# High and low input halves as one 512-column matmul in a two-block transformer kernel, with three changes of order

## What is computed

```python
# first block
xn = _rms(x, norm_attn)
fq, fk, fv, f_logit, nq, kc, vc, ks, vs, kw, vw, nsa_gate, gate_a, gate_b = split(xn @ w_in)
o_a = fox_attention(...)        # 8 heads of 128, decayed softmax
o_b = nsa_attention(...)        # 8 heads, compressed, selected and window branches
merged = sigmoid(gate_a) * (o_a @ w_up_fox) + sigmoid(gate_b) * (o_b @ w_up_nsa)
x = x + merged @ w_out
hn = _rms(x, norm_ffn)
x = x + (silu(hn @ w_ffn_gate) * (hn @ w_ffn_up)) @ w_ffn_down     # d_ff 5632
# second block, on 272 tokens: h = h + rmsnorm(mixer(rmsnorm(h))) for two mixers
#   group-query attention, 8 key groups, gated, then @ attn_w_out
#   gated linear attention, 4 heads, forward and backward, then @ gla_w_out
return h[:, 16:]
```

## Time and profile before

| | us |
|---|---|
| median of 3 runs | 2478.36 |
| lowest, highest | 2477.81, 2478.53 |
| profiled execution, its own time | 2478.49 |
| span of the profile | 2476.7 |
| mean granted TensorE clock | 0.995 |

### The profile page before, as it was taken

How to read it: one execution, slowest core, us unless ns; L and a number is a source line. 1 busy time by engine, 2 the same in 40 slices (tenths; PEclk the granted TensorE clock), 3 DMA queues, 4 the chain that set the end, 5 groups by cost and what they waited for, 6 DMA issues and landing times.

```text
span 2476.7 us, 50606 instructions
## 1 busy us (share of the span) xinstructions
PE 2440.7 (99%) x19618; PEld 2390.2 (97%) x19618; DVE 1474.9 (60%) x2213; ACT 1170.3 (47%) x1654; POOL 90.2 (4%) x117
## 2 busy tenths in 40 slices
PE   9999999999999999999999999999999989999997
PEld 8999999999999999999999999999999979999997
DVE  6666867655665555455554556555565466755655
ACT  6555554433545444334433445554454345545542
POOL 0000000000011000000000001000000100000001
PEclk9999999999999999999999999999999999999998
DMA  7546884466666666666666657655554545645553
GB/s 257 160 154 170 235 208 116 119 173 171 178 191 176 190 181 192 186 181 187 182 192 176 189 161 211 174 140 156 143 158 118 165 112 154 164 136 143 153 154 101
DMA packets 750272, 415.20 MB, mean 168 GB/s; under 512 B 44368, under 2 KB 738640, under 8 KB 750160
## 3 DMA queue, kind: packets, MB, share of 16 engines
q1 hardware_dynamic: 749328, 411.29, 59.3%
q10 hardware_dynamic: 832, 2.36, 0.2%
HBM read 408.35 MB, written 2.10 MB: 166 GB/s over the span
## 4 chain that ended last, share of the span: by engine, by line
PE 92%; DVE 4%; issue 2%; ACT 2%; DMA 0%; DVEq 0%; ACTq 0%; SPq 0%
PE ps_unit L254 27%; PE ps_unit L252 27%; PE ps_unit L253 27%; DVE w_lo L238 1%; PE ps_score L1018 1%; ACT w_hi L231 1%; PE ps_norm L863 0%; PE ps_out L863 0%; DVE work L355 0%; DMA raw<-in_w_fox 0%; PE ps_score L585 0%; PE ps_score L586 0%; DVE work L2548 0%; PE ps_score L842 0%; PE ps_score L817 0%
## 5 line engine op out<-in xcount | busy, mean ns | idle before, releaser
L238 DVE TENSOR_TENSOR w_lo<-raw,w_hi 128x1024 fp32r<-128x1024 f32 (+1 forms) x748 | 875.6, 1211 | 232.7 <-ACT w_hi L231 232.2
L231 ACT ACTIVATE w_hi<-raw 128x1024 fp32r<-128x1024 f32 (+1 forms) x768 | 777.0, 1042 | 440.6 <-PE ps_unit L254 436.8
L252 PE MATMUL ps_unit<-b_hi,w_hi 128*128 128x256 f32 (+1 forms) x3168 | 905.4, 286 | 2.0 <-DVE w_lo L238 2.0
L254 PE MATMUL ps_unit<-b_hi,w_lo 128*128 128x256 f32 (+1 forms) x3168 | 900.4, 284 | 0.0
L253 PE MATMUL ps_unit<-b_lo,w_hi 128*128 128x256 f32 (+1 forms) x3168 | 898.9, 284 | 0.0
L252 PE MATMUL ps_unit<-a_hi,w_hi 128*128 128x256 f32 (+1 forms) x2736 | 778.0, 284 | 3.8 <-DVE w_lo L238 3.4
L253 PE MATMUL ps_unit<-a_lo,w_hi 128*128 128x256 f32 (+1 forms) x2736 | 772.2, 282 | 0.0
L254 PE MATMUL ps_unit<-a_hi,w_lo 128*128 128x256 f32 (+1 forms) x2736 | 772.1, 282 | 0.0
L252 PEld LDWEIGHTS ps_unit<-b_hi,w_hi 128*128 128x128 f32 x3168 | 597.9, 189 | 7.5 <-issue 5.1
L254 PEld LDWEIGHTS ps_unit<-b_hi,w_lo 128*128 128x128 f32 x3168 | 598.5, 189 | 0.0
L253 PEld LDWEIGHTS ps_unit<-b_lo,w_hi 128*128 128x128 f32 x3168 | 595.7, 188 | 0.7
(11 more groups left out here) (385 smaller groups left out, 1704.4 us busy)
## 6 DMA issues: line engine op xcount, KB each, us to landing
raw<-in_attn_w_in SPq DMA_DIRECT2D x96, 512.0 KB, 4.8
raw<-in_gla_w_in SPq DMA_DIRECT2D x96, 512.0 KB, 4.5
raw<-in_w_in SPq DMA_DIRECT2D x88, 512.0 KB, 4.8
raw<-in_w_ffn_gate SPq DMA_DIRECT2D x88, 512.0 KB, 4.8
raw<-in_w_ffn_up SPq DMA_DIRECT2D x88, 512.0 KB, 4.8
raw<-in_w_fox SPq DMA_DIRECT2D x64, 512.0 KB, 4.3
raw<-in_w_ffn_down SPq DMA_DIRECT2D x64, 512.0 KB, 4.6
raw<-in_w_out SPq DMA_DIRECT2D x32, 512.0 KB, 4.5
```

The source lines that it names most:

```text
L231: act.activation(hi[:, b % 4, 0:size], raw[:, b % 8, 0:size], ACT.Copy)\
L238: dve.tensor_tensor(lo[:, b % 4, 0:size], raw[:, b % 8, 0:size], hi[:, b % 4, 0:size], ALU.subtract).then_inc(lo_ready, 1)
L252: pe.matmul(dst, wh, xh[:, k0 + k, 0:N], start=start and k == 0, stop=False)
L254: mm = pe.matmul(dst, wl, xh[:, k0 + k, 0:N], start=False, stop=stop and k == kb - 1)
```

## The change

The tiles AH and AL become the two halves of one tile A2, and BH and BL of B2. A matmul function gets that tile in place of the two. Where it is called with N = 2 * T (512), one matmul takes high and low input as 2 x 256 columns and writes the two halves of a bank; the third matmul adds to the first half. The two halves are added when the bank is evacuated, by a tensor_reduce and a multiply in evac_both, by two additions in add_to_x, or by a tensor_reduce alone in y_evac. Calls with N = T or TM stay at three matmuls.

```diff
-                pe.matmul(dst, wh, xh[:, k0 + k, 0:N], start=start and k == 0, stop=False)
-                pe.matmul(dst, wh, xl[:, k0 + k, 0:N], start=False, stop=False)
-                mm = pe.matmul(dst, wl, xh[:, k0 + k, 0:N], start=False,
+                if N == 2 * T:
+                    pe.matmul(dst.rearrange("p (a n) -> p a n", a=2), wh, x2[:, :, k0 + k, 0:T],
+                              start=start and k == 0, stop=False)
+                    mm = pe.matmul(dst[:, 0:T], wl, x2[:, 0, k0 + k, 0:T], start=False,
+                                   stop=stop and k == kb - 1)
+                    continue
+                pe.matmul(dst, wh, x2[:, 0, k0 + k, 0:N], start=start and k == 0, stop=False)
+                pe.matmul(dst, wh, x2[:, 1, k0 + k, 0:N], start=False, stop=False)
+                mm = pe.matmul(dst, wl, x2[:, 0, k0 + k, 0:N], start=False,
                                stop=stop and k == kb - 1)
...
+        def evac_both(dve, U, n, i, dst, added, count, ps=None):
+
+            ps = psU[U % 2] if ps is None else ps
+            dve.tensor_reduce(dst, ps[:, :].rearrange("p (a n) -> p n a", a=2), AX, ALU.add)\
+               .then_inc(added, 1)
+            dve.wait_ge(added, count)
+            dve.tensor_tensor(dst, dst, RS[:, 0:T], ALU.mult).then_inc(evacuated, 1)
...
-            dve.tensor_tensor(ch(X, kc, T), psU[U % 2][:, 0:T], ch(X, kc, T), ALU.add)\
+            ps = psU[U % 2]
+            dve.tensor_tensor(ch(X, kc, T), ps[:, T:2 * T], ch(X, kc, T), ALU.add).then_inc(added, 1)
+            dve.wait_ge(added, count)
+            dve.tensor_tensor(ch(X, kc, T), ps[:, 0:T], ch(X, kc, T), ALU.add)\
                .then_inc(evacuated, 1)
...
+            if both:
+                dve.tensor_reduce(ch(y, 4 * i + s, N), ps[:, :].rearrange("p (a n) -> p n a", a=2), AX,
+                                  ALU.add)\
+                   .then_inc(evacuated, 1)
```

Three changes of order go with it. In the q pair:

```diff
-                    nsa_turn(pe, n)
                     nsa_scores(pe, n + 1, g, 1)
+                    nsa_turn(pe, n)
...
+                    nsa_slope(dve, cb, n + 1)
                     nsa_copy_d(dve, n)
-                    nsa_softmax(dve, cb, n + 1)
+                    nsa_softmax(dve, cb, n + 1, False)
```

In the up-projection and at the last group of the group attention (the same is done on VectorE with split_lo, ahead of ga_gated):

```diff
+                    split_hi(act, U_UP + s + 1, 4, i)
                     act.activation(gates(j), gates(j), ACT.Sigmoid).then_inc(up_sg, 1)
-                    split_hi(act, U_UP + s + 1, 4, i)
...
             ga_copy_a(act, GQ_KV - 1)
+            split_hi(act, U_AO + 2, 4, 0)
             act.wait_ge(aq_pr, GQ_KV)
...
             for s in range(4):
-                if s:
+                if s >= 2:
                     split_hi(act, U_AO + s + 1, 4, 0)
```

179 lines of the change are left out of this document (99 added, 80 removed).

## The result

| | before | after |
|---|---|---|
| median, us | 2478.36 | 2463.14 (2462.51 to 2463.41) |
| ratio | | 0.9939, 95% interval 0.9927 to 0.9951 |
| span of the profile, us | 2476.7 | 2461.2 |
| mean granted TensorE clock | 0.995 | 0.995 |

The change is faster by 15.2 us, where 36.3 were forecast. The sign is right and the time lies in the forecast's range, but less than half of the gain came.

The account below looks back on a forecast made before the run. TensorE, busy 99%, bounds the kernel, so only shorter chunks or fewer gaps help. 40.5 us won by chunks less 5.0 and 8.1 of waits leaves 27.4; orders add 8.9: 2478.5 to 2442 us, range 2412 to 2474.

Parts of the forecast that it names:

- 3648 chunks: All wide matmuls: time beyond 2.4 GHz column pace belongs to the instruction, 225.5 ns against 236.6, 40.5 us won; chance 0.50.
- Fox, waiting: Seven Fox passes: two longer evacuations and earlier PE exceed the slack, 0.7 us of waiting a pass, 5.0 us lost.
- last FFN pass, waiting: Last FFN down pass: second addition makes VectorE's ring 4.71 us against PE's 4.13, 8.1 us lost over 14 units.
- q pairs: Scores moved ahead of the turn cover PE's wait for softmax weights; 2.8 us won over three passes.
- up-projection: Split moved ahead of the sigmoid, whose table load goes behind the split; 1.9 us won over three passes.
- last group's chain and clock: Splits made earlier remove PE's gap, 2.6 us won; 1.6 more if the clock then stays up.
- two separate halves of the operand cost a start each: Rival for the wide matmul: nothing won in the chunks, 2477 us; chance 0.12, shared with excess wholly by column.
- partly by column: Rival for the wide matmul: only 2.5 ns go of each instruction, 9.1 us in all, total 2469 us; chance 0.15.
- Hidden load: Rival: a long stream hides the weight load, 20.3 ns won a chunk, 74 us, total 2413 us; chance 0.10.
- The ring of the FFN pair: FFN gate and up: VectorE's 9.25 us becomes 10.67 with both additions, under PE's new 11.0, so hidden.
- The point from which it decides: FFN gate and up: VectorE's cover is gone once the addition to an evacuation exceeds about 0.87 us.
- Costed at nothing: w_out, gates, first two down passes and linear attention: enough idle time ahead of their evacuations, so no loss.

Follow-up runs that it names:

- e1: Matmuls alone on one core, 48 of each form, reference's work left out; 512 columns took 231.9 ns in two pieces, 226.9 in one, 256 columns 120.0.
- e12: Matmuls alone, 64 chunks of each form, varying stride, weight tiles and start; one piece and a narrow matmul took 353.3 ns a chunk at stride 512, 348.4 at 544.
- e8: The changed kernel with each tensor_reduce in the FFN's gate and up units done twice; 2496.05 us, ratio 1.0075 to the kernel before.
- e3: The changed kernel with the three changes of order put back, so wide matmuls alone; 2471.28 us, ratio 0.9971 to the kernel before.
- e6: The changed kernel with ACT's loop over the up-projection written out; 2461.34 us, ratio 0.9932 to the kernel before.
- e2: The kernel before with the three changes of order alone, all matmuls narrow; 2470.46 us, ratio 0.9969 to the kernel before.
- e9: Matmuls alone, 80 chunks of each form, weights in two tiles, three forms repeated beside busy ACT and VectorE; one piece took 348.5 ns a chunk without that traffic.
- e14: Matmuls alone, the same 48 chunks at stride 512 fifteen times, each behind other matmuls; six streams took 346.7 ns a chunk, nine 353.3.
- e15: Changed kernel with narrow last FFN pass, new Fox order, up-projection loop written out, one-piece operand; stride 512 in FFN only, 544 elsewhere; 2457.97 us, ratio 0.9922.
- e13: Changed kernel with narrow last FFN pass, new Fox order, up-projection loop written out, one-piece operand; stride 512 throughout the first block; 2453.45 us, ratio 0.9914.

## Why the prediction was right in sign and wrong in size

| step | forecast, us | measured, us |
|---|---|---|
| 3648 chunks | -40.5 (11.1 ns each) | -21.4 (5.9 ns each) |
| Fox, waiting | +5.0 | +4.0 |
| last FFN pass, waiting | +8.1 | +6.2 (+5.1 net, and 192 x 5.9 ns) |
| q pairs | -2.8 | -2.6 |
| up-projection | -1.9 | -0.9 |
| last group's chain and clock | -2.6 - 1.6 | -4.2 |
| not in the sum | 0 | +3.4 |
| span | -36.3 | -15.5 |

**The failed step is the price of the wide matmul.** The reading that the excess belongs to the instruction, and not to the column, was right: e1 has 13.3 ns at 256 and 13.6 at 512. The price was not: 225.5 ns were put in, and the wide matmul takes 230.8 in the kernel. These 5.3 ns, 3648 times, are 19 us, nearly all of what is missing; the narrow one behind it takes its 118.3. Two parts of it can be told apart. First, the excess was taken as one number, 12.2, from three narrow matmuls in turn, where the wide one at its best has 13.4 (226.7): 1.2 ns. Secondly, at this layout it has 17.5 (230.8 - 213.3). The other 4.1 ns go with the address pattern: wide ones alone take 231.9 in two pieces at stride 272 (e1), 231.9 in one piece at stride 528 and 230.0 at 544 (e12). What makes them inside the engine stays open. In the kernel one piece at stride 544 brought back 0.8 of the whole chunk.

The rival "two separate halves of the operand cost a start each" put the price at a full start, 11.1 ns more than mine; the two forms of e1 differ by 4.9, those of the kernel by 0.8, and the stride changed with them, so that such a cost isn't shown at all. The rival "partly by column" came near the time (2469) for a reason that e1 refutes. The price that really came lay between two of my cases, 225.5 and 236.6. That the range of 2412 to 2474 held the time is owed to the rivals that stretched it, and so in part to luck: my own case was given 2428 to 2456, too narrow for a price no row showed.

**A regular chunk.** At stride 512, begun at its first column, most forms are a multiple of 6.67 ns, that is 16 columns at 2.4 GHz: 120 = 18, 226.7 = 34, 346.7 = 52, 353.3 = 53, and 320 and 384 columns are at 22 and 26. That is N/16 + 2 such steps for each instruction. It is a fit to these rows, no mechanism shown; 448 columns (30.4 steps) and 128 (16.6 where it gives 10) don't fit it. By it three narrow ones (54) against a wide and a narrow one (52) are worth 13.3 ns, near the 11.1 of the forecast. The kernel gets 5.9 because its narrow ones were better than the fit, and its wide ones are worse.

**Hidden load.** The Trainium skill's rule of N/2.4 + 2.5 ns ("TensorE: Matmul & The Clock Gate", "Back-to-back issue gap") makes the wide one 215.8, an estimate by that page; no wide one here has a pace below 226.7, so for float32r the traces disagree with it at 512 columns as they did at 256.

**VectorE.** Tensor_reduce took 0.69 us where 0.68 was taken from the operation on 512 elements. The Trainium skill's sentence that it is the slowest operation ("VectorE: DVE Perf Modes", "Rules for kernel authors") isn't borne out at this shape. The ring of the FFN pair was right within 0.2 us, as e8 showed. The point from which it decides is an addition of 0.71 + 0.35 = 1.06 us to an evacuation, where 0.87 was forecast.

**Fox and the last pass.** Both waits were where they were foreseen. They are smaller since PE came sooner by less: in Fox by 0.28 us in place of 0.53, which turns the 0.71 of the prediction into 0.46, and 0.57 was measured. In the last pass the ring is 4.60 and not 4.71, and PE's need 4.19 and not 4.13.

**The orders.** The q pair and the chain are right to 0.2 us in the profiled executions. The clock's share of the chain, 1.6 forecast and 1.5 measured, is right by luck: its condition was that the clock stays up once the gap is gone, but in e3 it stayed up with the gap in place. The up-projection gave half. The step that failed was "the load goes with the sigmoid, behind the split": one load did, and a new one came ahead of the split, at the loop's top. e6 shows it.

**Costed at nothing, and not nothing.** Of the 3.4 us, 0.5 lie in the keys and values, 1.6 in the first head of the linear attention and 0.7 in the first part of its output projection (each counted against what its wide chunks should win), 0.2 ahead of the first Fox pass; the rest is rounding of the price per chunk. e3 shows them and e2 doesn't, so they come with the wide matmuls. In the first head PE waits twice in after and not at all before:

```profile
PE ps_unit L258 <- DVE w_lo L238: 0.7, 1, 0.7
PE ps_score L1148 <- DMA con<-in_gla_gk_up: 0.4, 1, 0.4
```

Ahead of the third unit of the output projection it waits 0.7 us for VectorE's evacuation, where it was 0.3. The rest of that 0.7, and the keys and values, were not followed.

## What to carry to other kernels

A price that no row shows should be measured alone before a sum of 3648 of them is built on it; where it can't be, the case's own range must reach to the next rival. An operation lengthened beside a busy engine is covered only up to the wait for that engine inside its ring. Neither the idle share nor the slack of the product at the consumer says that: VectorE was idle for 31% of that stretch in after, its product 0.8 us early, and e8 still lost 0.75 us a pair. And where a table switch is moved in a loop, look at what the first activation of the body finds loaded.

## What was not expected of the hardware

- The pace of float32r matmuls goes with the address pattern of the moving operand at full clock. 512 columns took 226.7 ns at strides of 512 and 640 columns, 226.9 at 576 and 231.9 at 528 (e12; one stream each but for 512), and at a stride of 272 the steps repeat with k, round after round (225 to 235 ns for the wide ones in two pieces, 113 to 125 for the narrow ones, in e9). How much of this is what ran ahead, as in the next point, wasn't tried.
- At stride 512 the same stream of 512 and 256 columns has two lasting states, 346.7 and 353.3 ns a chunk. What ran ahead of it sets the state: one narrow matmul more or less is enough (e14). It costs 1.9% of a stage, at granted clock 1.00. Whether a stage of a kernel falls the same way in every execution isn't shown: e15's five executions lie within 0.8 us, but one of e13's six is 12 us above the rest. What the states are inside the engine stays open.
- 512 columns in two pieces took 4.9 ns more than in one, and in four pieces 12.3 more, alone; 2.1 or 0.8 beside narrow matmuls. The address pattern changed with the pieces, and the two effects are not told apart.
- The granted clock fell to 0.50 behind a gap of 2.53 us on PE in the trace before, and stayed at 1.00 behind one of 2.52 us at the same place in e3.
- 128 columns took 110.6 ns (e1), over twice the 53.3 of its columns at 2.4 GHz, and only 9.4 less than 256 columns.
